# Q and K as token rows turned by PE, modulation sums in other DVE steps, and another split of the last tile

## The reference

```
cond = silu(c)
for i in range(2):
    sh_m, sc_m, g_m, sh_f, sc_f, g_f = split(cond @ mod_w[i] + mod_b[i], 6)
    h = x * (1 + sc_m) + sh_m
    y = attention(h, w_qkv, w_o) if i == 0 else short_conv(h, ...)
    x = layer_norm(ALPHA * x + (1 + g_m) * y, ln_g[i, 0], ln_b[i, 0])
    h = x * (1 + sc_f) + sh_f
    y = square(relu(h @ w1 + b1)) @ w2 + b2
    x = layer_norm(ALPHA * x + (1 + g_f) * y, ln_g[i, 1], ln_b[i, 1])
```

## Time and profile before

| | |
|---|---|
| median of three runs | 2220.59 us (2220.35 to 2221.53) |
| the profiled execution | 2218.09 us, its span 2216.2 us |
| granted TensorE clock | 1.00 of full speed |
| PE busy | 2176.3 us, 98% |
| DVE busy | 1758.6 us, 79% |
| ACT busy | 1127.6 us, 51% |
| DMA | 650.41 MB, mean 293 GB/s |
| the chain that ended last | PE 87%, DVE 6%, DMA 3% |

### The profile page before, as it was taken

The page is one execution under the profiler, slowest core; times in us unless marked ns, Lnnn a source line. Parts: engine busy times, 40 slices in busy tenths (PEclk is TensorE's granted clock), DMA queues, the critical chain, the costliest instruction groups (busy, mean ns, idle before and its releaser), DMA issues.

```text
span 2216.2 us, 27554 instructions
## 1 busy us (share of the span) xinstructions
PE 2176.3 (98%) x10446; PEld 1832.1 (83%) x10446; DVE 1758.6 (79%) x1804; ACT 1127.6 (51%) x1403; POOL 7.1 (0%) x25
## 2 busy tenths in 40 slices
PE   5999999999999999999999999999999999999998
PEld 5999988888888888888878888888888888888886
DVE  7899999977988988999988898667666666655667
ACT  4777875365345435435455433337544543543552
POOL 0000000000000000000000000000000000000000
PEclk9999999999999999999999999999999999999999
DMA  9999998869999999999958988766787787866672
GB/s 353 385 386 396 398 376 300 283 231 351 394 347 325 370 341 321 360 344 335 335 175 295 332 295 286 235 205 212 255 295 232 249 277 231 265 212 190 203 265 100
DMA packets 317043, 650.41 MB, mean 293 GB/s; under 512 B 31840, under 2 KB 63088, under 8 KB 315248
## 3 DMA queue, kind: packets, MB, share of 16 engines
q1 hardware_dynamic: 313568, 634.73, 83.2%
q10 hardware_dynamic: 3344, 13.93, 1.6%
HBM read 623.15 MB, written 2.12 MB: 282 GB/s over the span
## 4 chain that ended last, share of the span: by engine, by line
PE 87%; DVE 6%; DMA 3%; issue 2%; ACT 1%; SPq 1%; ACTq 0%; DVEq 0%
PE bank L1439 25%; PE bank L1440 25%; PE bank L1441 25%; PE bank L1429 3%; PE bank L1432 3%; PE bank L1431 3%; DMA mod_raw<-in_mod_w 2%; DVE mod_acc L984 1%; DVE w_low L1069 1%; PE bank L1447 1%; PE bank L1451 1%; PE bank L1446 1%; DMA stage<-stage 1%; DMA raw<-in_attn_w_qkv 0%; SPq L559 0%
## 5 line engine op out<-in xcount | busy, mean ns | idle before, releaser
L719 ACT ACTIVATE w_high<-raw 128x1024 fp32r<-128x1024 f32 x752 | 788.0, 1059 | 966.2 <-PE bank L1441 910.7
L1069 DVE TENSOR_TENSOR w_low<-raw,w_high 128x1024 fp32r<-128x1024 f32 x752 | 912.5, 1222 | 354.8 <-ACT w_high L719 353.6
L1439 PE MATMUL bank<-w_high,h_high 128*128 128x512 f32 x1632 | 636.5, 390 | 3.0 <-DVE w_low L1069 3.0
L1440 PE MATMUL bank<-w_low,h_high 128*128 128x512 f32 x1632 | 635.0, 389 | 0.0
L1441 PE MATMUL bank<-w_high,h_low 128*128 128x512 f32 x1632 | 635.0, 389 | 0.0
L984 DVE SCALAR_TENSOR_TENSOR mod_acc<-mod_raw,cond,mod_acc 128x1024 f32<-128x1024 f32 x345 | 442.2, 1282 | 23.5 <-DMA mod_raw<-in_mod_w 20.6
L1439 PE MATMUL bank<-w_high,hid_high 128*128 128x512 f32 x1048 | 408.1, 389 | 2.3 <-DVE w_low L1069 2.3
L1441 PE MATMUL bank<-w_high,hid_low 128*128 128x512 f32 x1048 | 407.7, 389 | 0.0
L1440 PE MATMUL bank<-w_low,hid_high 128*128 128x512 f32 x1048 | 407.7, 389 | 0.0
L1439 PEld LDWEIGHTS bank<-w_high,h_high 128*128 128x128 f32 x1632 | 306.4, 188 | 68.2 <-issue 3.8
L1441 PEld LDWEIGHTS bank<-w_high,h_low 128*128 128x128 f32 x1632 | 306.4, 188 | 63.7
(11 more groups left out here) (156 smaller groups left out, 1176.6 us busy)
## 6 DMA issues: line engine op xcount, KB each, us to landing
raw<-in_mlp_w SPq DMA_DIRECT2D x512, 512.0 KB, 5.7
mod_raw<-in_mod_w SPq DMA_DIRECT2D x368, 512.0 KB, 8.2
raw<-in_attn_w_qkv SPq DMA_DIRECT2D x96, 512.0 KB, 10.6
raw<-in_conv_w_in SPq DMA_DIRECT2D x96, 512.0 KB, 5.7
stage<-stage SPq DMA_DIRECT2D x176, 128.0 KB, 2.9
raw<-in_attn_w_o SPq DMA_DIRECT2D x32, 512.0 KB, 8.2
raw<-in_conv_w_out SPq DMA_DIRECT2D x32, 512.0 KB, 4.7
mod_raw<-in_mod_w SPq DMA_DIRECT2D x32, 256.0 KB, 6.5
```

Source lines behind the costliest of these rows:

```text
L719: act.activation(chunk_slots(n)[0], raw[:, n % NCH], ACT.Copy).then_inc(high_done, 1)
L1069: dve.tensor_tensor(low_, raw[:, n % NCH], high.bitcast(F32), ALU.subtract).then_inc(raw_used, 1)
L1439: pe.matmul(dst, high[:, k, c], wh, start=first, stop=False, skip_group_check=True)
L1440: pe.matmul(dst, high[:, k, c], wl, start=False, stop=False, skip_group_check=True)
```

## The change

- Q and K are computed by token rows, as V. `visit_banks` puts each token tile's 128 tokens x 512 features into `q_t` or `k_t` in four pieces of 128 columns. In the last round, after the two chunks that follow a group's last one, PE turns the four 128x128 blocks of one token tile each (`turn_qk`) into bank 6, and ACT copies them back over the rows (`take_turned`). PE turns the next four only when that copy is done (`qk_out`). The scores of head 0 wait for group 4's copies, those of head 1 for all sixteen; the latter move from after chunk 89 to after chunk 90.
- `light_step` moves a block's turn to the next step with a place for it, and the partial sum to the next such step behind it; the fold, the finish and the gate's line and row follow the partial sum at the distance that they had. The tiles of blocks 11 to 20 are spread over steps 148 to 363 instead of 148 to 371. Of the ten turns there, they go from steps 172, 190, 214, 238, 256, 284, 305, 323, 350, 371 to 175, 191, 213, 239, 255, 277, 303, 319, 341, 367; the four later ones from 423, 469, 600, 671 to 423, 471, 605, 679.
- Of the last token tile only quarter 0 goes over PE. Quarter 1 is scaled by ACT in place, and POOL adds the bias. SP sends out in the order 2, 1, 0, 3.

```
+    QK_VISITS = [N_VISITS - QKV + g for g in range(QK)]
+    QK_TURN_AT = {LAST_CHUNK[v] + 1 + t: (g, t) for g, v in enumerate(QK_VISITS) for t in range(TT)}
...
-    SCORES_AT = {N_O - 10: 0, N_O - 7: 1, N_O - 2: 2}
+    SCORES_AT = {N_O - 10: 0, N_O - 6: 1, N_O - 2: 2}
...
+    def light_step(n):
+        while True:
+            w, j = divmod(n - SLOTS, NCH)
+            if w in (W_MLP[0] + 1, W_MLP[1] + 1):
+                light = ()
+            elif W_CIN <= w < W_COUT:
+                light = (3, 4)
+            else:
+                light = (1, 2) if w in UNIT_GROUPS else (3, 4, 5, 6)
+            if j in light:
+                return n
+            n += 1
...
-    for n0, n1, b1 in ((N_MLP0 + 2 * NCH + 4, W_TAIL[1] * NCH + 20, block_of(UNITS + SCALE_F)),
+    for n0, n1, b1 in ((N_MLP0 + 2 * NCH + 4, W_TAIL[1] * NCH + 12, block_of(UNITS + SCALE_F)),
...
-                TURN_AT[n], PART_AT[n + 1], FOLD_AT[n + 2 + NCH], MOD_AT[n + 6] = b, b, b, b
+                turn = light_step(n)
+                part = light_step(turn + 1)
+                TURN_AT[turn], PART_AT[part], FOLD_AT[part + 1 + NCH], MOD_AT[part + 5] = b, b, b, b
...
-        BY_PE = 2
+        BY_PE, BY_POOL = (0,), (1,)
...
+        qk_ps = bank[6]
...
-                for q in range(NG):
+                for q in range(NG) if t < TT - 1 else (2, 1, 0, 3):
...
+            for q in BY_POOL:
+                rows = res[:, TT - 1, cols(q)]
+                pool.wait_ge(rows_in, 32 * LNS)
+                pool.wait_ge(out_scaled, 1)
+                pool.tensor_tensor(rows, rows, b_last[:, cols(q)], ALU.add).then_inc(out_pool, 1)
...
-                rows = flat((q_t, k_t)[g // NG][:, g % NG * GT:(g % NG + 1) * GT, :])
-                return [(start_ps(v)[b][:, :], rows[:, b * 2 * T:(b + 1) * 2 * T]) for b in range(2)]
+                rows = (q_t, k_t)[g // NG][:, g % NG * GT:(g % NG + 1) * GT, :]
+                return [(start_ps(v)[t][:, :].rearrange("p (m n) -> p m n", m=GT), rows[:, :, toks(t)])
+                        for t in range(TT)]
...
+            def take_turned(g, t):
+                act.wait_ge(qk_turned, TT * g + t + 1)
+                act.activation((q_t, k_t)[g // NG][:, g % NG * GT:(g % NG + 1) * GT, toks(t)],
+                               qk_ps[:, :].rearrange("p (m n) -> p m n", m=GT), ACT.Copy).then_inc(qk_out, 1)
...
+                if n - SLOTS - 1 in QK_TURN_AT:
+                    take_turned(*QK_TURN_AT[n - SLOTS - 1])
                 if n in visit_at:
                     v = visit_at[n]
                     take_out(v)
...
-            for q in range(BY_PE):
+            for q in BY_POOL:
+                act.wait_ge(out_mean, t * NG + q + 1)
+                act.activation(res[:, t, cols(q)], res[:, t, cols(q)], ACT.Identity, scale=roots[:, t, 1:2]
+                               ).then_inc(out_scaled, 1)
+            for q in BY_PE:
...
+            def turn_qk(g, t):
+                pe.wait_ge(parts_out, sum(goes_on(u) for u in range(2, QK_VISITS[g] + 3)))
+                if g or t:
+                    pe.wait_ge(qk_out, TT * g + t)
                 for m in range(GT):
+                    rows = (q_t, k_t)[g // NG][:, g % NG * GT + m, toks(t)]
+                    ins = pe.transpose(qk_ps[:, m * P:(m + 1) * P], rows, ident[:])
+                ins.then_inc(qk_turned, 1)
...
+                elif s < LEAD - 1:
+                    pe.wait_ge(qk_out, TT * QK if s else TT * (NG + 1))
...
-                    if g < QK:
-                        ins = feature_row(start_ps(v), r * GT + k, wh[:, kk, :], wl[:, kk, :], begins, ends)
-                    else:
-                        for t in range(TT):
-                            ins = token_row(v % 2, t, r * GT + k, wh[:, kk, :], wl[:, kk, :], h_high, h_low,
-                                            begins, ends)
+                    for t in range(TT):
+                        ins = token_row(v % 2, t, r * GT + k, wh[:, kk, :], wl[:, kk, :], h_high, h_low,
+                                        begins, ends)
                 ins.then_inc(chunk_mult, 1)
+                if n in QK_TURN_AT:
+                    turn_qk(*QK_TURN_AT[n])
```

More of the change, by code:

```diff
@@ L210, in build_trunk @@
                 b = done // KT
-                TURN_AT[n], PART_AT[n + 1], FOLD_AT[n + 2 + NCH], MOD_AT[n + 6] = b, b, b, b
+                turn = light_step(n)
+                part = light_step(turn + 1)
+                TURN_AT[turn], PART_AT[part], FOLD_AT[part + 1 + NCH], MOD_AT[part + 5] = b, b, b, b
                 if is_gate(b):
-                    LINE_AT[n + 7 + NCH], ROW_AT[n + 9 + NCH] = b, b
+                    LINE_AT[part + 6 + NCH], ROW_AT[part + 8 + NCH] = b, b
         assert done == last
@@ L342, in build_trunk @@
         parts_out = sem("parts_out")
+        qk_turned = sem("qk_turned")
+        qk_out = sem("qk_out")
         post_done = sem("post_done")
@@ L393, in build_trunk @@
         out_done = sem("out_done")
+        out_scaled = sem("out_scaled")
+        out_pool = sem("out_pool")
         diag_done = sem("diag_done")
@@ L601, in _ @@
             for t in range(TT):
-                for q in range(NG):
-                    if t == TT - 1 and q < BY_PE:
+                for q in range(NG) if t < TT - 1 else (2, 1, 0, 3):
+                    if t == TT - 1 and q in BY_PE:
                         sp_.wait_ge(out_copied, q + 1)
+                    elif t == TT - 1 and q in BY_POOL:
+                        sp_.wait_ge(out_pool, 1)
                     else:
-                        sp_.wait_ge(out_done, NG * t + q + 1 - (BY_PE if t == TT - 1 else 0))
+                        sp_.wait_ge(out_done, NG * t + q + 1 - (len(BY_PE + BY_POOL) if t == TT - 1 else 0))
                     sp_.dma_start(o_rows[:, t, cols(q)], res[:, t, cols(q)]).then_inc(out_dma, 16)
@@ L1387, in _ @@
                         newton(n, t)
-                    if t == TT - 1 and q < BY_PE:
+                    if t == TT - 1 and q in BY_PE + BY_POOL:
                         continue
@@ L1422, in _ @@
             turn_x(0)
-            def feature_row(dsts, k, wh, wl, first, last):
+            def turn_qk(g, t):
+                pe.wait_ge(parts_out, sum(goes_on(u) for u in range(2, QK_VISITS[g] + 3)))
+                if g or t:
+                    pe.wait_ge(qk_out, TT * g + t)
                 for m in range(GT):
-                    c = slice(m * P, (m + 1) * P)
-                    dst = dsts[m // 2][:, T * (m % 2):T * (m % 2 + 1)]
-                    pe.matmul(dst, wh[:, c], h_high[:, k, :], start=first and m % 2 == 0, stop=False,
-                              skip_group_check=True)
-                    pe.matmul(dst, wh[:, c], h_low[:, k, :], start=False, stop=False, skip_group_check=True)
-                    ins = pe.matmul(dst, wl[:, c], h_high[:, k, :], start=False, stop=last,
-                                    skip_group_check=True)
-                return ins
+                    rows = (q_t, k_t)[g // NG][:, g % NG * GT + m, toks(t)]
+                    ins = pe.transpose(qk_ps[:, m * P:(m + 1) * P], rows, ident[:])
+                ins.then_inc(qk_turned, 1)
             def token_row(par, t, k, wh, wl, high, low, first, last):
```

## The result

The changed kernel takes 2225.06 us (median of 14 runs, 2224.00 to 2227.67); the kernel before, run beside it, 2220.36 us (14 runs, 2217.12 to 2221.55). The ratio is 1.0022, with a 95% interval of 1.0014 to 1.0029: slower by 4.7 us, 0.2%. Forecast was 2228.6 us within 2220.5 to 2233.0, slower. So the sign and the range held, and the size was some 3.5 us too large.

What follows compares the result with a forecast made beforehand. PE and DVE with its DMA stream were taken as near-equal bounds of the QKV stage. Terms 10.5 - 2.3 - 0.2 = +8.0 us gave 2226.1 us profiled, 2228.6 us carried to the median, range 2220.5 to 2233.

Steps and rivals of the forecast that it cites:

- The loop of DVE and the DMA stream: QKV stage: tile loads and DVE pace each other without PE, running just ahead of PE, almost the same bound.
- (a): QKV chunks before 74: 8.0 us less PE work, but PE must await DVE's low half; -0.3 us, bounds 0 and -8.0.
- The 2 us that I named as refuting it: Chunk 74: the prediction is wrong if PE passes it more than 2 us earlier than 248.6.
- (b): Chunks 74 to 87, the other 14 of Q and K: shorter PE work counts in full, -2.2 us.
- (c): Last QKV round: 64 PE transposes of 128x128 between chunks, nothing hiding them, +7.0 us.
- (d): Last QKV round: PE waits for ACT's copy out of bank 6 eight times, 0.75 us each, +6.0 us.
- Light steps: Modulation sums moved to lighter steps: PE's wait for the low half of chunk 373 goes, -2.3 us.
- the hidden-layer copy near 1075 us: Next late item after chunk 373's stall; it waits for the swap DMAs and was claimed unchanged by the edit.
- my bound was 1.5: Steps 148 to 363: extra tiles in some twelve steps cost 0, at most +1.5 us where DVE is just in time.
- The last tile: End of kernel: quarter 1 over ACT and POOL, quarter 2's issue earlier, frees a queued wait; -0.2 us.
- my bounds of 0.22 and 7: Last tile: limits in us for POOL's 128x512 add, taken as 1.1 us.
- Rival D: End of kernel: DVE's two-operand instructions lock POOL out until 2212.6; +1.5 for -0.2, 2230.3 us, chance 0.07.

Runs made afterwards that it cites:

- e4: The changed kernel without the 64 transposes and ACT's 16 copies (scores left wrong): 2214.88 us against 2219.53 for the kernel before, ratio 0.9978.
- e8: The changed kernel loading only half of each modulation tile in steps 6 to 89, DVE's adds unchanged: 2219.10 us, ratio 0.9994 to the kernel before.
- e9: The changed kernel with DVE adding only half of each modulation tile in steps 6 to 89, loads whole: 2224.62 us in one execution.
- e3: The changed kernel with ACT's copy of a group's second token tile right after the put-back, before the high half: 2218.01 us, ratio 0.9992 to the kernel before.
- e2: The kernel before with only the modulation sums in light steps and tiles spread to step 363: 2217.21 us against 2219.53, ratio 0.9988.
- e5: The kernel before with only the new division of the last tile: 2219.53 us against 2219.43, ratio 0.9999.
- e11: The kernel before, unchanged, timed and profiled a second time: 2220.89 us against 2219.79, ratio 1.0002; profiled execution 2221.90 us.
- e1: The changed kernel with the old modulation steps and old last tile, only Q and K as token rows left: 2230.57 us against 2219.53, ratio 1.0046.
- e10: The changed kernel with POOL writing zeros over quarter 1 instead of adding the bias: end 11.83 us after PE's last low-half product started, for 12.27.
- e6: The kernel before with eight extra PE products ahead of the wait for root_diag at the end: 2222.95 us, ratio 1.0013.
- e7: e2 with eight extra PE products ahead of the wait for root_diag at the end: 2219.76 us, ratio 1.0000 to the kernel before.

## Why the prediction was right, and where it was off

**What bounds the kernel: right, and now shown.** The loop of DVE and the DMA stream does not contain PE (e4), and within it the transfers are the bound (e8 against e9). The prediction left open which of the two it was.

**(a) Chunks before 74, forecast -0.3: right in kind.** Measured -1.0, of which -0.8 were there at chunk 6. I had taken the slack from one chunk's row and not looked at the start; that the tile stream is not yet the bound there is likely, and no run tested it. Between chunks 6 and 74 the edit gave 0.2 us. The 2 us that I named as refuting it were not reached.

**(b), (c) and (d), forecast -2.2 + 7.0 + 6.0 = +10.8: measured +12.5 from chunk 74 to 92.** (d) is 6.6 us in starts: seven waits of 0.83 to 0.87 us and one of 0.74, against 8 x 0.75. e3 puts the price of the whole wait at 7.2 by the starts at chunk 95, and at 6.2 by the medians. What (b) and (c) leave in e3, from -1.3 to +4.4, is 5.7 us against 4.8. Some 0.2 of the 0.9 between them is the batches of four transposes, which cost 0.45 us each and not 0.44, and 0.5 are products, which start 0.230 us apart here instead of 0.2275; the rest is not placed, nor why the products are slower. Together (a) to (d) are +11.5 for +10.5.

**Light steps, forecast -2.3: measured -3.6 from chunk 352 to 373.** 2.5 us of them are the stall at chunk 373, as reasoned. The step that failed is "the hidden-layer copy near 1075 us ... the edit leaves". PE gains another 0.6 to 1.5 us at chunks 358 and 359 in every version with light steps, and its wait of 0.5 us for that copy (`hid_high`) is gone. The DMA view from 1055 to 1085 us (busy tenths, GB/s, then the swap DMAs with their time to landing) shows how, first of before, then of e2:

```profile
DMA  5000069899988999899999999999999999999999
GB/s 208 19 0 0 0 87 221 295 385 351 174 229 180 292 363 328 257 371 404 392 378 395 400 385 388 393 393 407 388 399 407 393 385 401 407 393 391 377 363 399
...
stage<-stage SPq DMA_DIRECT2D x4, 128.0 KB, 6.7
```

```profile
DMA  9999999999789999999999999999999999999999
GB/s 412 407 399 407 382 325 360 399 407 298 262 251 322 352 344 352 410 401 391 388 370 350 310 341 352 369 385 396 374 347 407 401 412 415 423 380 404 366 404 396
...
stage<-stage SPq DMA_DIRECT2D x4, 128.0 KB, 4.9
```

Before, DVE had a block's turn, its partial sum and the residual of a token tile ahead of one low half, which came at 1056.68 us; the load of the chunk that takes that slot held SP's queue for up to 5.2 us. The DMA engines stood still for some 3 us, and what had piled up, two chunks, four tiles and the four DMAs of a fold, was then sent just ahead of the swap DMAs, which took 6.7 us to land. With the new steps the turn and the partial sum lie elsewhere, the engines never stop, and the swaps land in 4.9. I had costed a late low half only by PE's wait for it, not by SP's, whose queue carries everything else. That this makes the copy late was read from the traces; no run moved the fold or the turn alone. The price that I feared in the denser steps exists and is small: after and e9 show 0 and 0.6 us at chunks 176 and 177, the other versions with light steps 0.4 to 1.7 us there; my bound was 1.5.

**The last tile, forecast -0.2: measured +0.4 in the profiles, and 0 in the medians of e5 (-2.2 to +1.8 us).** POOL's add takes 1.65 us, not 1.1; my bounds of 0.22 and 7 held it, and 1.1 may be right for the part of it that does not lie beside DVE's scaling. Rival D had the right mechanism and half of its order: I let DVE lock POOL out to the end, since DVE's last four instructions leave hardly a gap. POOL is held up by one of them at the most, and the next one then has to wait for POOL. That costs DVE 1.0 us. Some 0.6 come back behind it: quarter 3's issue starts 0.03 us after DVE is done instead of 0.32, and its transfer lands in 2.58 us instead of 2.90. The step that failed here is that the add would cost DVE nothing.

**From the profile to the median: the step that made the forecast too large.** The sum from the profile was +8.0 us, and 2226.1 us for a profiled execution; it came to +7.5 us and 2225.55. Then I carried +8.0 over to the median, as if the edit moved every execution alike. It does not. Before has three places where executions differ, and its profiled one was quick at all: the clock between 41 and 45 us (1.0 us in e11), the wait at chunk 431 (0.4 us there, 1.9 in e11) and the end (11.88 and 13.16). After's profile shows none of the three losses: its median and its profile are 0.5 us apart, where before's are 2.3. 11.5 for Q and K, less 3.6 for the light steps, less 0.7 to 2.1 at chunk 431, and an end from 0.4 us longer to 0.9 shorter make 4.9 to 7.6 us; against e11's execution, which also began 1.0 us later, after is 3.65 us slower. The 4.7 of the medians lies between. What a typical execution of before does at the three places is worked out from the two profiles of it and from those that share its code there, and not counted over many.

**What stays open.** Why PE does not wait at chunk 431 any more. All six profiles with turned Q and K (after, e1, e3, e8, e9, e10) gain 0.65 us there against before. The six others (e2, e4, e5, e6, e7, e11) do not and lose 0.2 to 1.8 us, the most in e4, with token rows and no turns. So it is not the time by which the stage moves: e3 stands near before's times and has no wait. DVE's wait for tiles between 1236 and 1275 us is smaller in after:

```profile
DVE mod_acc L1029 <- DMA mod_raw<-in_mod_w: 1.1, 3, 0.7
```

In the profile of before it is 2.6 us, in e11's 3.3, in e1's 1.8. That points to when the transfers land, and no run here changed that alone.

## What to carry over

When an edit lightens an engine that shows no idle time, look for a second stream just behind it, and test that stream's limit by halving its bytes and its work apart; here the transfers, not a DVE busy for 96%, held back six of the eight microseconds saved on PE (e8). A copy of 0.6 us, made sixteen times, can cost 7 if it stands behind work that is not urgent: before moving work to an engine with spare time, write down its queue order at each place and let what the bottleneck waits for go first. Before adding a difference from one profile to a median, find where executions of the old kernel differ from each other, for an edit can remove that too.

## What the runs showed of the hardware

- A POOL addition of 128x512 float32, begun beside one two-input DVE instruction, takes 1.65 us, and the next, issued 0.44 us after it, takes 1.76 us instead of 0.75 (after; 1.64 and 1.75 in e5). A POOL write of the same size takes 0.52 us beside such an instruction and delays nothing (e10).
- A float32 product of 512 columns takes 0.86 us at 2.4 GHz, in two records of 0.43: eight products, sixteen records, in 6.9 us (e6). Those on `fp32r` parts start 0.227 us apart.
- After 2.7 us without work for PE at the end of the kernel the granted clock was 2.4 GHz in two profiles of the old last tile and mostly 1.2 in two others; four matmuls took 1.98 us or 3.3 to 3.5. With 3.6 us without work it was also either: 1.2 GHz in after, e8 and e10, where the remaining two took 2.07 us, partly so in e9 (1.62 us), and 2.4 GHz in e3, e4 and e5 (1.12 us). After and e5:

```profile
2216.62 2.07 PE L1748 MATMUL bank<-res,stage 128*128 128x512 f32 x2 [3.60 <-ACT stage L977]
```

```profile
2210.88 1.13 PE L1719 MATMUL bank<-res,stage 128*128 128x512 f32 x2 [3.60 <-ACT stage L947]
```

The window of after at its two:

```profile
2216.60:2218.70 2.10, 2.07 (x2) 0.50 (x2) 2.06 (x4) 0.72 (x1) 0.86 (x1) 0.50 0.00 0
```
